# A two-layer model on one core: two thirds of the modulation product moved under the recurrence, attention two pairs ahead, smaller blocks in two triangular inversions

## The reference, cut to what matters

```python
# first layer
proj = rmsnorm(x) @ w_in                 # u, qkv, z, beta, alpha, gates
br_s5 = glu(s5_branch(u) @ s5_glu_w)     # complex diagonal scan
# chunk_gated_delta_rule, chunks of 64 tokens, 8 heads of 128
lmat = where(strict, (k_beta @ k.T) * decay, 0)      # 64 x 64
sol  = triangular_solve(eye + lmat, rhs)             # unit lower
attn = where(tril, (q @ k.T) * decay, 0)
x = x + merged @ w_out
x = x + (silu(act) * val) @ ffn_down
# second layer
mod = silu(c) @ ada_w + ada_b            # ada_w: 2048 x 12288, 96 MB
mod_c = silu(c_ctx) @ ada_w + ada_b
sh1, sc1, g1, sh2, sc2, g2 = split(mod, 6)
z = modulate(rmsnorm(x, norm1_g), sh1, sc1) @ w_in   # and zc from ctx
attn = windowed_gqa(q, k, v, kc, vc, sink)           # 16 heads of 64, 4 kv heads
#   s = q k' / 8 + mask; m = max(s, sink)
#   p = exp(s - m) / (sum exp(s - m) + exp(sink - m)); out = p v
# rwkv: per head of 64, forward and backward, first over ctx, then over x
#   S = S * w + (S . -kk) (kk a)' + v k';  y = S . r
x = x + g1 * (concat(attn, rw) @ w_out)
x = x + g2 * swiglu(modulate(rmsnorm(x, norm2_g), sh2, sc2))
```

## Time and profile before

| | us |
|---|---|
| median of 3 runs | 3700.38 (3689.09 to 3700.86) |
| the profiled execution's own time | 3704.32 |
| its span | 3702.5 |
| PE busy | 3484.8 (94%), 28666 instructions |
| DVE busy | 2379.7 (64%) |
| ACT busy | 1693.0 (46%) |
| DMA | 572 MB, 154 GB/s over the span |
| mean granted clock of PE | 0.97 |

### The profile page before, as it was taken

The page is one execution under the profiler, slowest core; times in us unless marked ns, Lnnn a source line. Parts: engine busy times, 40 slices in busy tenths (PEclk is TensorE's granted clock), DMA queues, the critical chain, the costliest instruction groups (busy, mean ns, idle before and its releaser), DMA issues. The chain is left out here.

```text
span 3702.5 us, 74594 instructions
## 1 busy us (share of the span) xinstructions
PE 3484.8 (94%) x28666; PEld 2955.7 (80%) x28666; DVE 2379.7 (64%) x4144; ACT 1693.0 (46%) x2572; POOL 109.9 (3%) x159
## 2 busy tenths in 40 slices
PE   9999998997899999999899997888788899999998
PEld 8998886877788888888788965776676788888887
DVE  5759995666678878656633553776675666656555
ACT  5547772223455555444312434444443455555343
POOL 0000000000000000000000001211110000000000
PEclk9999998998999999999999998999998999999999
DMA  5547774443455555555322464000002455555553
GB/s 200 180 137 292 266 275 165 163 167 137 159 182 181 181 181 181 193 187 187 113 101 92 158 228 159 6 8 7 8 5 105 159 181 183 188 187 187 172 185 134
DMA packets 83113, 572.03 MB, mean 154 GB/s; under 512 B 9584, under 2 KB 11888, under 8 KB 18128
## 3 DMA queue, kind: packets, MB, share of 16 engines
q1 hardware_dynamic: 81216, 560.60, 42.8%
q0 software_dynamic: 1680, 8.36, 0.6%
HBM read 566.82 MB, written 2.10 MB: 154 GB/s over the span
## 5 line engine op out<-in xcount | busy, mean ns | idle before, releaser
L252 DVE TENSOR_TENSOR w_lo<-raw,w_hi 128x1024 fp32r<-128x1024 f32 x880 | 1037.0, 1199 | 272.0 <-ACT w_hi L245 262.5
L245 ACT ACTIVATE w_hi<-raw 128x1024 fp32r<-128x1024 f32 (+1 forms) x877 | 894.5, 1037 | 613.7 <-PE po L287 310.1
L286 PE MATMUL po<-hh,w_hi 128*128 128x512 f32 x2816 | 1001.4, 400 | 20.8 <-DVE hh L391 9.5
L287 PE MATMUL po<-hh,w_lo 128*128 128x256 f32 x2816 | 790.8, 281 | 0.0
L286 PEld LDWEIGHTS po<-hh,w_hi 128*128 128x128 f32 x2816 | 530.3, 188 | 164.0 <-issue 18.7
L287 PEld LDWEIGHTS po<-hh,w_lo 128*128 128x128 f32 x2816 | 533.4, 189 | 0.0
L286 PE MATMUL po<-ff,w_hi 128*128 128x512 f32 x1408 | 499.0, 399 | 7.9 <-DVE ff L1836 7.9
L287 PE MATMUL po<-ff,w_lo 128*128 128x256 f32 x1408 | 396.6, 282 | 0.0
L286 PEld LDWEIGHTS po<-ff,w_hi 128*128 128x128 f32 x1408 | 265.9, 189 | 73.0 <-issue 8.5
L287 PEld LDWEIGHTS po<-ff,w_lo 128*128 128x128 f32 x1408 | 267.9, 190 | 0.0
L266 PE MATMUL po<-hh,w_lo 128*128 128x256 f32 x928 | 266.0, 287 | 0.4 <-DVE w_lo L252 0.4
(11 more groups left out here) (577 smaller groups left out, 6369.1 us busy)
## 6 DMA issues: line engine op xcount, KB each, us to landing
raw<-ffn_up SPq DMA_DIRECT2D x176, 1024.0 KB, 4.8
raw<-w_in SPq DMA_DIRECT2D x112, 1024.0 KB, 4.9
raw<-ada SPq DMA_DIRECT2D x86, 1024.0 KB, 6.6
raw<-ffn_down SPq DMA_DIRECT2D x64, 1024.0 KB, 5.0
raw<-w_out SPq DMA_DIRECT2D x32, 1024.0 KB, 4.9
raw<-ffn_down SPq DMA_DIRECT2D x32, 768.0 KB, 4.3
raw<-glu SPq DMA_DIRECT2D x16, 1024.0 KB, 5.9
ada_third<-ada SPq DMA_DIRECT2D x10, 1024.0 KB, 6.6
```

Of the source, the lines that this page charges most:

```text
L245: act.activation(w_hi[:, k % 4, 0:width], raw[:, k // 2 % ring, (k % 2) * PW:(k % 2) * PW + width], ACT.Copy).then_inc(hi_ready, 1)
L252: dve.tensor_tensor(w_lo[:, k % 4, 0:width], raw[:, k // 2 % ring, (k % 2) * PW:(k % 2) * PW + width], w_hi[:, k % 4, 0:width].bitcast(F32 ...
L286: pe.matmul(halves(bank), hi, pair[:, :, t, :], start=first and n == 0, stop=False)
L287: mm = pe.matmul(po[bank][:, 0:T], lo, pair[:, 0, t, :], start=False, stop=last and n == len(tiles) - 1)
```

## The change

Four parts.

1. **Modulation.** `ADA_S5, ADA_LATE = 8, 16`: 8 blocks stay, under S5. The 16 blocks that are needed late (64 MB) come as 128 pieces of 512 KB, 64 columns each, through two slots `ada_late` during the recurrence: 8 pieces and 2 turns into columns a unit, one of them in each of its 10 half-steps, between PE's wait for DVE's result of e = 0 and that for e = 1. PE gets `late_pe`, DVE `late_dve` (copy of 256 columns, addition into `mod`), SP `modulation`, whose load of piece k + 2 waits for piece k's product; the `k_w` loads are put between these. `DN_ADA`, `ada_third` and the chunks in `att_pe` are gone.
2. **Recurrence's inversion.** Levels 1 to 4 (8 of 10 half-steps) go from `blocks_pe` to `quads_pe`: 32 products of 32x32 on the four diagonal tiles, four for e = 0 into `pa`, four for e = 1 into `po`, and so on. Level 5 stays.
3. **Attention.** Scores two pairs ahead. DVE does mask, scaling, sink and maximum in one `tensor_tensor_reduce`. The pieces of the exponentials are turned by transposes and not normalised; `t_dg` is gone. The value product has `t_pt` as weights (128 columns) and `t_v` as moving data (64 columns); its output is multiplied by 1/sum on DVE, turned by two transposes a pair (`att_turn_pe`) and copied by ACT. `t_pt` is doubled.
4. **Delta rule.** All triangles are kept as 64x64 blocks, [4,64]; `halves_pe` does a half-step as 8 products of 64x64 on alternating row tiles in one bank; one set in place of two. The mask load and two memsets differ accordingly.

```diff
-        ADA_S5, ADA_DN, ADA_ATT = 10, 6, 8
+        ADA_S5, ADA_LATE = 8, 16
...
+        def halves_pe(pe, by_pe, out, lhs, rhs):
+            for m in range(4):
+                for r in (slice(0, C), slice(C, P)):
+                    o, w = out[r, m * C:m * C + C], rhs[r, m, :]
...
+                    mm = pe.matmul(o, lhs[r, m, :], w, start=True, stop=True)
+            mm.then_inc(by_pe, 1)
...
+        def quads_pe(pe, sets, outs, lhs, rhs, own):
+            settle(pe)
+            for m in range(4):
+                mm = []
+                for e in range(2):
+                    for g in range(4):
+                        r, h = slice(32 * g, 32 * g + 32), g % 2 * 32
+                        c = h if own else 0
+                        last = pe.matmul(outs[e][r, m * C + c:m * C + c + 32], lhs[e][r, m, h:h + 32],
+                                         rhs[e][r, m, c:c + 32], start=True, stop=True)
+                    mm.append(last)
...
+        def late_pe(pe, j, x, s):
+            h, c = s // 5, s % 5
+            if c < 4:
+                k = 4 * h + c
+                pe.wait_ge(late_landed[k % 2], j * 128 + ((64 if x == "l" else 0) + 16 * (k // 2) + 16))
+                settle(pe)
+                o = T + 64 * c
+                for n in range(KD):
+                    t = n % 4
+                    mm = pe.matmul(inv_bank[0][32 * t:32 * t + 2, o:o + 64], cve[:, n, :], ada_late[:, k % 2, n, :],
+                                   start=n < 4, stop=n >= 12)
+                mm.then_inc(late_p[x].did(f"c{k}"), 1)
+            else:
+                pe.wait_ge(*late_v[x].at(j, f"r{h}"))
+                settle(pe)
+                for m in range(2):
+                    mm = pe.matmul(inv_bank[0][:, T + 2 * m:T + 2 * m + 2], ada_late_row[:, m * P:m * P + P], ada_sel[:],
+                                   start=True, stop=True)
...
+        def inv_mask_pe(pe, n, sets, l, between=None):
             for by_pe, by_dve, (i_a, i_t, i_tt, i_p), b, want in sets:
                 pe.wait_ge(by_dve, n * 17 + (3 * l if l == 1 else 3 * l - 1))
+                if between is not None and want == "tt":
+                    between(2 * l - 2)
...
+            if l < 5:
+                quads_pe(pe, sets, outs, lhs, rhs, True)
+            else:
+                blocks_pe(pe, n, sets, 2 * l - 1, outs, lhs, rhs)
...
+            def modulation(j, x, part, last=False):
+                for k in part:
+                    sp.wait_ge(*late_p[x].at(j, f"c{k}"))
+                    settle(sp)
+                    if k < 6:
+                        late(j * 2 + (x == "l"), k + 2)
+                    elif not last:
+                        late(j * 2 + (1 if x == "c" else 2), k - 6)
```

In the attention of `att_pe`:

```diff
             for n in range(4):
-                if b and n == 0:
-                    pe.wait_ge(ada_copied, ADA0 + b)
-                ada_chunk(pe, (ADA0 + b) * 4 + n, po[3])
-                pe.wait_ge(*agv.at(b, f"g{n}"))
+                pe.wait_ge(*aea.at(b, f"p{n}"))
...
                 for kb in range(4):
-                    mm = pe.matmul(po[n % 2][:, kb * P:kb * P + P], t_s[b % 2][:, n, kb * P:kb * P + P], t_dg[:, n, :],
-                                   start=True, stop=True)
+                    mm = pe.transpose(turn_bank(b, n)[:, kb * P:kb * P + P], t_s[b % 2][:, n, kb * P:kb * P + P], ident[:])
...
+            if b < 6:
+                att_scores_pe(pe, b + 2)
...
-                    mm = pe.matmul(po[2][r, q0:q0 + P], t_v[:, kb, vcol], t_pt[:, n, kb, :],
-                                   start=kb == 0, stop=kb == 3)
+                    mm = pe.matmul(out_bank(b)[:, (2 * h + a) * 64:(2 * h + a) * 64 + 64], t_pt[b % 2][:, n, kb, :],
+                                   t_v[:, kb, vcol], start=kb == 0, stop=kb == 3)
```

More of the change, by code:

```diff
@@ L1021, in rows_pe @@
             yield
[L1025 to L1036, removed]
@@ L1092, in lower @@
+            for l in range(1, 6):
+                inv_mask_dve(dve, n, sets, l, d_mask)
+                yield
+                inv_sum_dve(dve, n, sets, l)
+                yield
         def lower(ap, b, first=0):
@@ L1129, in inv_sum_pe @@
+        def inv_sum_pe(pe, n, sets, l, between=None):
             for by_pe, by_dve, (i_a, i_t, i_tt, i_p), b, want in sets:
                 pe.wait_ge(by_dve, n * 17 + (3 * l + 1))
+                if between is not None and want == "tt":
+                    between(2 * l - 1)
             lhs = [i_p if l == 5 and want == "tt" else i_tt for _, _, (i_a, i_t, i_tt, i_p), b, want in sets]
             rhs = [i_tt if l == 5 and want == "tt" else i_p[:, :, 0:C // 2] for _, _, (i_a, i_t, i_tt, i_p), b, want in sets]
-            blocks_pe(pe, n, sets, 2 * l, [s[3][1] for s in sets], lhs, rhs)
@@ L1154, in inv_mask_dve, with inv_sum_dve @@
                        .then_inc(by_dve, 1)
-        def inv_sum_dve(dve, n, sets, l):
+        def inv_sum_dve(dve, n, sets, l, between=None):
             w = 2 ** l
@@ L1176, in program @@
         DN_TURNS = 27
-        DN_SPAN = 4 * DN_TURNS
-        DN_ADA = {}
-        for _b in range(ADA_DN):
-            _t = _b * DN_SPAN // ADA_DN
-            for _c in range(4):
-                DN_ADA[_t + 3 * _c] = ("chunk", 4 * (ADA_S5 + _b) + _c)
-            DN_ADA[_t + 10] = ("row", ADA_S5 + _b)
-            DN_ADA[_t + 12] = ("columns", ADA_S5 + _b)
-            DN_ADA[_t + 14] = ("read", ADA_S5 + _b)
         def dn_in(i):
@@ L1307, in dn_pe, with chunks @@
             q, k, v = dn_in(i)
+            def chunks(out, lhs, rhs, name):
+                for a in range(2):
+                    for t in range(2):
+                        for r in range(2):
+                            o, s = (2 * a + t) * C, slice(t * P + r * C, t * P + r * C + C)
+                            mm = pe.matmul(out[r * C:r * C + C, o:o + C], lhs[:, a, s], rhs[:, a, s], start=True, stop=True)
+                mm.then_inc(dnp.did(name), 1)
             def each(fn, name):
@@ L1327, in dn_pe @@
             pe.wait_ge(*dnv.at(i, "kb"))
-            each(lambda a, t, m, s: pe.matmul(pa[0][:, m], k[:, a, s], d_kb[:, a, s], start=True, stop=True), "kk")
-            each(lambda a, t, m, s: pe.matmul(pa[2][:, m], k[:, a, s], q[:, a, s], start=True, stop=True), "kq")
+            chunks(pa[0], k, d_kb, "kk")
+            chunks(pa[2], k, q, "kq")
             yield
@@ L1701, in att_scores_pe, with turn_bank, out_bank, att_turn_pe @@
                   .then_inc(asp.did(f"s{n}"), 1)
[L1703 to L1706 removed]
+        def turn_bank(b, place):
+            return po[(5 * b + place) % 2]
+        def out_bank(b):
+            return po[2 + b % 2]
+        def att_turn_pe(pe, b, bank):
+            pe.wait_ge(*agv.at(b, "o"))
+            for h in range(2):
+                mm = pe.transpose(bank[:, h * P:h * P + P], t_o[b % 2][:, h * P:h * P + P], ident[:])
+            mm.then_inc(otp.did("o"), 1)
```

394 lines of the change are left out of this document (186 added, 208 removed).

## The result

The changed kernel takes **3814.85 us** (median of 4 runs, 3799.49 to 3827.17), the kernel before 3700.62: a ratio of 1.031, 95% interval 1.026 to 1.035. It is 114 us slower. I had forecast 3631, and a range that ended at 3692.

A forecast was written before the change was run, and what follows sets the result against it. PE was taken to bound S5, delta rule and attention, and a chain of waits the recurrence, with room on PE and idle memory. Terms -9 - 48 - 53 + 40 = -70 gave 3631 us, range 3590 to 3692.

The forecast's parts named there:

- S5: S5 scan stage: two modulation blocks less take 9.7 us off PE, counted as -9.
- Delta rule: Delta rule and GLU: six modulation blocks less and cheaper products sum to -52, with 4 us given back -48.
- the half-step: Delta rule's inversion: 40 half-steps, each from 0.90 to 0.46 us as 16 instructions in two row tiles, -17.6 us.
- Attention: Attention stage: modulation chunks gone, a pair of heads from 14.40 to 8.2 us, the stage from 126.3 to 73, -53.
- Recurrence: Recurrence: late pieces and turns added, inversion tiles shortened, DVE +10 and landings +9, together +40.
- the tiles' term: Recurrence's inversion: 128 half-steps on 32x32 tiles at 0.46 in place of 0.93 us, -58 of PE time, times 0.65.
- the pieces' and turns': Recurrence's late modulation on PE: pieces +73 and turns +18 before the 0.65 share, plus DVE +10 and landings +9.
- 0.65 of any PE time: Recurrence: share of added or removed PE time taken to show in the total, chosen from 94 of 149 us.
- one bank taking one row tile at a time: Rival (a), recurrence and delta rule: a half-step on 32x32 tiles takes 1.86 us, total 3764; chance 9%.
- starts no closer than 25 ns: Recurrence rival: 64 starts take 1.6 us and a piece 0.8, +121 on part 4, total 3751; chance 3%.
- My sign of being wrong: Recurrence's half-step L1089 above 1.1 us; also ada_late waits over 20 us or an attention pair above 10 us.
- Rival (c): Recurrence: pieces cost more through late landings, full PE or half clock; part 4 +67 to +97, total 3658 to 3688; 15%.

The follow-up runs named there:

- the run with tiles alone: Changed kernel with the late modulation's pieces, turns, copies and loads left out, 32x32 inversion tiles kept: 3663.3 us, 0.989 of before.
- 113 measured alone: Changed kernel with the recurrence's inversion back on 64x64 blocks at all levels, late pieces kept: 3721.72 us, 1.005 of before.
- the doubled half-steps: Changed kernel without late modulation, on 64x64 blocks, each half-step's 16 products made twice: 3727.6 us, 1.008 of before.
- the base: Changed kernel with neither the late modulation nor the 32x32 tiles: 3598.0 us, 0.972 of before.
- wide products and blocks: Changed kernel with pieces of four 256-column products and the inversion on 64x64 blocks: 3694.43 us, 0.997 of before; measured again, 3690.86.
- the pieces ahead of the wait: 64x64 blocks, four 256-column products a piece, six of a unit's eight pieces put before PE's wait for DVE: 3685.4 us, 0.9945 of before.

## Why the prediction was wrong

**S5** (-9): the stage went from 278.2 to 271.1, -7; right.

**Delta rule** (-48): -37 in the stage, 266.2 to 229.1 us. The step that was mis-sized is the half-step. Its 16 product instructions do take 0.46 us in two row tiles of one bank, as worked out, but from its first start to the next line's it is 0.61: 0.15 us pass from its last start to that, and the start ahead of it is 0.1 us later than usual too. So going into 64x64 tiles and back costs about 0.1 us each way, which I had not put in:

```profile
590.37 0.68 PE L1022 MATMUL pa<-i_p,i_tt 64*64 64x64 f32 x16
590.98 0.39 PE L567 MATMUL po<-ys_hi,w_lo 128*128 128x256 f32 x1
```

Before, start to next start, the half-steps come to 34.1 us in sum, after to 24.5: 9.6 us in place of 17.6. That is 8 of the 11 us missing; it holds the old half-step too, 0.85 us and not 0.90.

**Attention** (-53): 126.3 to 71.9 us, -54.4; right, with two small misses that cancel. A full pair takes 8.6 us against the 8.2 worked out, and the last two pairs, whose scores are already made, 6.5, which I had not seen. The transposes wait for ACT's copies as said (0.34 and 0.20 us), and the values take 3.62 us where they took 3.26: half the moving columns, with twice the weight columns, saved nothing.

**Recurrence** (+40): +228, and here the prediction fell. What failed is that an instruction was priced by its time in the array alone: the supply of instructions had no term, and the clock none. Of the 188 us missed, some 95 are the tiles' term (-38 forecast, +57 measured alone), 35 the pieces' and turns' (0.65 x 91 + 19 = 78 forecast, 113 measured alone) and 57 what the two cost on top of each other, by the profiled executions. Term by term:

- Pieces and turns. Their array time was right at the full clock (a piece 0.56 us from its start to the next line's), but at 1.2 GHz it is 0.96, and in the full change at least 49 of the 128 ran there. The share "0.65 of any PE time" was too small: the doubled half-steps give 0.80, and they stand elsewhere on the chain than the pieces. With it, 0.8 x 91 = 73 us, and 19 us of issue waits over the base make 92 of the 113. The 9 us for landings did not come (PE waited 0.9 us for them in that run); the other 20 us, DVE's 10 among them, are not split.
- Tiles, -0.45 x 128 x 0.65 = -38. The half-step is nearly as fast as I said (0.56 us from first to last start at the full clock, priced 0.46, against 0.93 on blocks); at 1.2 GHz it is 0.84 and saves next to nothing. But the gain isn't there: alone it cost +57. A half-step on tiles is 128 instructions with their weight loads in half a microsecond; the fetch brings some 250 in about 1.0 us of transfer and 1.4 us until PE goes on. With it goes the low clock, 270 us of half speed in the run with tiles alone against 52 in the base.
- The two together: 192 instructions in 1.1 us at seven half-steps a unit. Issue waits of 100 us, 44 more than the two parts' sum, of an interaction of 57 in the profiled executions (31 by the medians).

**The rivals.** I put the slower outcome on one bank taking one row tile at a time (9%) and on starts no closer than 25 ns (3%). Both are out: 63 starts in 0.55 us, four row tiles on one bank. The 1.10 us that I gave as the point of decision was passed by 33 of the 128 half-steps, all with a wait for instructions inside; the others took 0.56 us at the full clock and 0.84 at 1.2 GHz. My sign of being wrong came, but not for the reason I had tied to it. Rival (c) named both things that happened, PE full so that 0.65 becomes 1, and the clock at half for longer, but capped them at +97, because the clock had no term of its own in it. The supply of instructions was in no rival, though the kernel before had its trace: at the loop's edges two waits of 2.3 and 2.0 us named "issue", inside stretches of 1.2 GHz that had begun 1 us before them. I had read them as the cost of a branch. The 15.7% "issue" of the earlier trace rows, 77 us, is a poor sign of it: only 6 us of that stretch were waits of PE of 0.15 us or more, and the base has 14.1% with 4 us.

**The rest.** The time after the recurrence, whose code is the same, was 872.4 us before and 858.5 after, and between 859.1 and 875.0 in the profiles of the experiments, without relation to the edit that I can see. I take it as scatter of single executions. The recurrence scatters too, by 15 us in the one kernel that was profiled twice, so a difference of that size between stages is not shown by them.

What stays open: how the interaction divides between fetch and clock, since in the full change most long waits for instructions were followed by the low clock and I have no run that holds it. Nor was it tried to take the fetch's delay away by itself.

## What to carry to other kernels

Moving work out of a full stage into a neighbour with idle time pays only if its price there is lower: under this recurrence a modulation block cost 96/16 = 6.0 us with wide products and blocks, and 5.3 us with the pieces ahead of the wait (its ratio less that of the run with neither edit, 0.0229, x 3706 / 16), in the full stages 4.9 (4 x 0.97 + 0.98). By this account the 0.5% that the best version gains comes from the other edits of the attention and the delta rule.

Of a large change, run the edits that touch one stage apart and together: two that cost 57 and 113 us alone cost 228 together in the profiled executions.

## What the runs showed of the hardware that was not expected

- The instruction fetch is visible as packets of 16 KB on its own queue, 148 in the recurrence after; PE resumes 1.2 to 1.6 us after the end of one, in 52 of 53 long waits. With the data's loads taken away the issue waits were 82 us instead of 100.
- The granted clock was 0.75 with products of 32 columns and 0.94 with 64 in the same tiles, with the same number of products and the same idle time of PE (92 us in both).
- Products of 32x32 on four diagonal tiles start 9 ns apart while all four row tiles write one bank. The Trainium skill, "TensorEngine Tiling (Array Packing)", Gotcha 1, says that different row tiles cannot use one bank at the same time; no run here shows such a limit in time.
- With 128x128 weights an instruction with 64 moving columns takes 3.62/32 = 0.113 us, no less than one with 128 in the prediction's reading of the earlier trace rows, 0.112.
